# Squares' sums on VectorE, weight rests after the rows, and gates emptied in pairs, in a two-block transformer kernel

## What is computed

```python
def rmsnorm(x, g):
    return x * lax.rsqrt(jnp.mean(x * x, axis=-1, keepdims=True) + EPS) * g

# first block: start, and its end
    h = rmsnorm(x, g_mix); z = h @ w_in
    ...
    gate = jax.nn.sigmoid(rmsnorm(x, g_ple) @ w_ple_gate)
    x = x + gate * (p @ w_ple_proj)
    return rmsnorm(x, g_final)

# second block
    h = rmsnorm_2(x, norm_mix_pre)
    proj = h @ w_in
    conv_in, q, k, v, g_conv, g_att = jnp.split(proj, splits, axis=-1)
    u = causal_depthwise_conv(glu(conv_in), w, b)        # 31 taps
    u = silu(layernorm_2(u, conv_ln_g, conv_ln_b))
    att = stick_breaking_attention(q, k, v)
    merged = sigmoid(g_conv) * (u @ w_cb + b) + sigmoid(g_att) * (att @ w_ab)
```

## Time and profile before

| | us |
|---|---|
| median of 3 runs | 964.51 |
| lowest, highest | 963.71, 965.91 |
| profiled execution, own time | 964.45 |
| its span | 962.7 |
| PE busy | 935.1 (97%) |
| DVE busy | 498.7 (52%) |
| ACT busy | 330.4 (34%) |
| POOL busy | 39.2 (4%) |

### The profile page before, as it was taken

How to read it: one execution, slowest core, us unless ns; L and a number is a source line. 1 busy time by engine, 2 the same in 40 slices (tenths; PEclk the granted TensorE clock), 3 DMA queues, 4 the chain that set the end, 5 groups by cost and what they waited for, 6 DMA issues and landing times.

```text
span 962.7 us, 14239 instructions
## 1 busy us (share of the span) xinstructions
PE 935.1 (97%) x5914; PEld 660.7 (69%) x5914; DVE 498.7 (52%) x869; ACT 330.4 (34%) x527; POOL 39.2 (4%) x39
## 2 busy tenths in 40 slices
PE   7999999999999899999999899999999999999997
PEld 6997734444444444443344499988889999999886
DVE  7784613222212322222132397997788987776642
ACT  6832211001101010100011367556456755644541
POOL 1000000000000000000000000222320000000000
PEclk9999999999999999999999999999999999999999
DMA  9987799999999999999999974442334424555301
GB/s 348 403 368 325 296 396 430 428 433 429 432 428 432 427 430 430 431 432 428 431 429 419 428 302 165 176 175 88 135 129 175 176 110 176 208 211 195 132 1 44
DMA packets 28982, 289.45 MB, mean 301 GB/s; under 512 B 3057, under 2 KB 6385, under 8 KB 12401
## 3 DMA queue, kind: packets, MB, share of 16 engines
q1 hardware_dynamic: 28192, 286.91, 72.9%
q10 hardware_dynamic: 720, 1.57, 0.4%
HBM read 287.43 MB, written 1.05 MB: 300 GB/s over the span
## 4 chain that ended last, share of the span: by engine, by line
PE 82%; DVE 6%; SPq 5%; ACT 3%; DMA 2%; issue 2%; POOL 0%; DVEq 0%; ACTq 0%
PE ps L279 81%; SPq L2244 5%; DVE wl L275 3%; DMA ring<-in_w_pg 2%; ACT wh L268 1%; PE ps L1063 1%; DMA arena<-in_xT 0%; DVE arena L1549 0%; ACT arena L1848 0%; DVE arena L1889 0%; DVE arena L1960 0%; DVE mg_l L1896 0%; DVE mix_l L606 0%; ACT arena L1851 0%; DVE arena L593 0%
## 5 line engine op out<-in xcount | busy, mean ns | idle before, releaser
L279 PE MATMUL ps<-ring,arena 128*64 128x512 f32 x1216 | 339.2, 597 | 4.8 <-issue 4.7
L275 DVE TENSOR_TENSOR wl<-ring,wh 128x1024 fp32r<-128x1024 f32 x150 | 180.5, 1235 | 49.4 <-ACT wh L268 49.3
L279 PEld LDWEIGHTS ps<-ring,arena 128*64 128x64 f32 x1216 | 109.5, 137 | 122.1 <-issue 120.3
L268 ACT ACTIVATE wh<-ring 128x1024 fp32r<-128x1024 f32 x150 | 151.7, 1051 | 48.5 <-PE ps L279 34.3
L279 PE MATMUL ps<-arena 128*64 128x512 f32 (+4 forms) x448 | 166.7, 523 | 0.9 <-DMA ring<-in_moe 0.4
L279 PEld LDWEIGHTS ps<-arena 128*64 128x64 f32 (+2 forms) x448 | 58.6, 144 | 89.6 <-issue 82.8
L1168 DVE SCALAR_TENSOR_TENSOR arena<-ps,arena 128x512 f32<-128x512 f32 x16 | 12.0, 751 | 202.6 <-PE ps L279 202.6
L279 PE MATMUL ps<-up_h,wh 128*128 128x256 f32 x352 | 85.5, 281 | 0.7 <-ACT up_h L1949 0.7
L279 PE MATMUL ps<-up_l,wh 128*128 128x256 f32 x352 | 82.1, 280 | 0.0
L1238 ACT ACTIVATE y_h<-ps 128x512 fp32r<-128x512 f32 x32 | 19.0, 596 | 151.9 <-PE ps L279 151.9
L279 PEld LDWEIGHTS ps<-up_h,wh 128*128 128x128 f32 x352 | 66.3, 188 | 0.9 <-issue 0.9
(11 more groups left out here) (275 smaller groups left out, 1487.6 us busy)
## 6 DMA issues: line engine op xcount, KB each, us to landing
ring<-in_moe SPq DMA_DIRECT2D x69, 2048.0 KB, 22.5
arena<-in_moe SPq DMA_DIRECT2D x17, 2048.0 KB, 22.4
ring<-in_w_in SPq DMA_DIRECT2D x12, 2048.0 KB, 10.6
ring<-in_w_up SPq DMA_DIRECT2D x11, 2048.0 KB, 7.6
ring<-in_moe SPq DMA_DIRECT2D x24, 512.0 KB, 15.1
ring<-in_w_dn SPq DMA_DIRECT2D x5, 2048.0 KB, 7.8
ring<-in_w_out SPq DMA_DIRECT2D x4, 2048.0 KB, 16.0
arena<-in_moe SPq DMA_DIRECT2D x8, 512.0 KB, 14.6
```

Source lines behind the costliest of these rows:

```text
L268: e.activation(wh(i), raw_piece(i), ACT.Copy).then_inc(*hi.up(i))
L275: e.tensor_tensor(wl(i), raw_piece(i), wh(i), SUB).then_inc(*lo.up(i))
L279: return e.matmul(o, l, r, start=first, stop=final, skip_group_check=True)
```

## The change

1. Start: all eight sums of squares stand ahead of the first product.
2. Gate projection: `norm3`'s eight matmuls go. VectorE adds the eight chunks of `SQ` up in three steps (`added`) and PE does one matmul on the result, behind `four`. The weight rests of pieces 6 and 7 move into VectorE's loop, the reciprocal of r3 to its head, and the rests of the second projection's first four pieces from the loop to behind it.
3. Second projection: `four_late` takes the place of `four`: both products with `wh` for all rows first, then the rests of the weights. The eight `ones` matmuls go: VectorE adds the squares up into `SUM4`, and one matmul into bank 3 stands ahead of Q's products; ScalarE copies it out, and its root is taken at the merge. The weight rests 5 to 7 stand behind R45's first use.
4. Attention: two gate projections share a bank and are emptied by one operation on 512 columns; the rest of piece 41 (counted from the second projection's first) moves to the merge.
5. Merge: the mean of the convolution takes block 3 first and waits for each block by itself.

```diff
...
+        def four_late(e, outs, name, n, xh, xl, ready, at):
+            i0 = n_piece[(name, n), 0]
+            for j in range(4):
+                e.wait_ge(*hi.at(i0 + j))
+            for c in range(8):
+                e.wait_ge(*ready.at(c))
+                for j in range(4):
+                    mm(e, outs[j], wh(i0 + j)[:, c, :], xh[:, c, :], c == 0, False)
+                    mm(e, outs[j], wh(i0 + j)[:, c, :], xl[:, c, :], False, False)
+                at(e, c)
+            for j in range(4):
+                e.wait_ge(*lo.at(i0 + j))
+                for c in range(8):
+                    k = mm(e, outs[j], wl(i0 + j)[:, c, :], xh[:, c, :], False, c == 7)
+                k.then_inc(*proj.up(name, n, j))
...
-        means = sig("means", ["r1", "r3", "r4", "r5", "mu", "var", "r6", "r7"])
+        means = sig("means", ["r1", "r3", "r5", "r4", "mu", "var", "r6", "r7"])
...
             e.wait_ge(*made.at("ones"))
-            squares((1, 0, 3, 2, 5))
-            three(e, ps[3][:, 0:256], "in1", 0, 0, XGH, XGL, xg, between=lambda: squares((7, 4, 6)))
+            squares((1, 0, 3, 2, 5, 7, 4, 6))
+            three(e, ps[3][:, 0:256], "in1", 0, 0, XGH, XGL, xg)
             for j in range(1, 4):
...
         scaled = sig("scaled", range(8))
+        sum3 = sig("sum3", ["four", "two", "all"])
+        sum4 = sig("sum4", ["four", "two", "all"])
+        SUM4 = RB[:, 1, :]
         gate = sig("gate", range(8))
...
-        def sums(e, c):
+        def sum_gained(e, c):
...
             e.wait_ge(*sq4.at(c))
-            a = mm(e, ps[6][:, 0:256], inv1024, SQ[:, c, :], c == 0, c == 7)
-            b = mm(e, ps[7][:, 0:256], gsq[:, c:c + 1].to_broadcast([128, 128]), SQ[:, c, :], c == 0, c == 7)
+            k = mm(e, ps[7][:, 0:256], gsq[:, c:c + 1].to_broadcast([128, 128]), SQ[:, c, :], c == 0, c == 7)
             if c == 7:
-                a.then_inc(*means.up("r4"))
-                b.then_inc(*means.up("r5"))
+                k.then_inc(*means.up("r5"))
+        def added(e, out, ready, steps):
+            e.wait_ge(*ready.at(7))
+            e.tensor_tensor(SQ[:, 0:4, :], SQ[:, 0:4, :], SQ[:, 4:8, :], ADD).then_inc(*steps.up("four"))
+            e.wait_ge(*steps.at("four"))
+            e.tensor_tensor(SQ[:, 0:2, :], SQ[:, 0:2, :], SQ[:, 2:4, :], ADD).then_inc(*steps.up("two"))
+            e.wait_ge(*steps.at("two"))
+            e.tensor_tensor(out, SQ[:, 0, :], SQ[:, 1, :], ADD).then_inc(*steps.up("all"))
...
         def ple_pe(e):
-            def norm3(e, c):
-                mean(e, ps[7][:, 0:256], SQ, inv1024, [sq3.at(x) for x in range(8)], "r3")
-            four(e, [ps[j][:, 0:256] for j in range(4)], "pgate", 0, XPH, XPL, ple, first=ple_h, at=norm3)
+            four(e, [ps[j][:, 0:256] for j in range(4)], "pgate", 0, XPH, XPL, ple, first=ple_h)
+            e.wait_ge(*sum3.at("all"))
+            mm(e, ps[7][:, 0:256], inv1024, SQ[:, 0, :], True, True).then_inc(*means.up("r3"))
             for j in range(4, 8):
...
                                        op0=M, op1=SUB).then_inc(*ple.up(c))
-            split_lo(e, FIRST + 8)
+            added(e, SQ[:, 0, :], sq3, sum3)
+            split_lo(e, FIRST + 6)
...
             for j in range(8):
-                if j == 1:
+                if j == 0:
                     recip(e, "r3", RB[:, 0, :])
                     e.wait_ge(*recips.at("r3"))
-                if j >= 1:
+                else:
                     scale(j - 1)
+                split_lo(e, FIRST + min(6 + j, 8))
                 if j >= 2:
...
                     parts(j - 3)
-                split_lo(e, FIRST + (8, 8, 9, 10, 12, 12, 12, 12)[j])
             scale(7)
...
             parts(7)
-            split_lo(e, FIRST + 16)
+            split_lo(e, FIRST + 13)
...
         gs_in = sig("gs_in", range(4))
+        r4m = sig("r4m", [0])
         gs_sig = sig("gs_sig", range(4))
...
         at_l = h5.then(range(4))
-        sg_in = sig("sg_in", range(16))
+        sg_in = sig("sg_in", range(8))
         chunks = [(n, j) for n in range(4) for j in range(4)]
...
                     for x in range(5):
-                        sums(e, x)
-                elif c == 6:
-                    for x in range(5, 8):
-                        sums(e, x)
-            four(e, [ps[j][:, 0:256] for j in range(4)], "in2", 0, H5H, H5L, h5, at=norms)
+                        sum_gained(e, x)
+                if c >= 5:
+                    sum_gained(e, c)
+            e.wait_ge(*scaled.at(3))
+            four_late(e, [ps[j][:, 0:256] for j in range(4)], "in2", 0, H5H, H5L, h5, norms)
             for j in range(4):
-                e.wait_ge(*(scaled.at(4 + j) if j < 2 else roots.at("r4" if j == 2 else "r45")))
+                e.wait_ge(*(scaled.at(4 + j) if j < 3 else roots.at("r45")))
                 three(e, ps[4 + j][:, 0:256], "in2", 1, j, H5H, H5L)
+            e.wait_ge(*gs_in.at(3))
+            e.wait_ge(*sum4.at("all"))
+            mm(e, ps[3][:, 0:256], inv1024, SUM4, True, True).then_inc(*means.up("r4"))
             for j in range(4):
-                e.wait_ge(*gs_in.at(j))
+                e.wait_ge(*(gs_in.at(j) if j < 3 else r4m.at(0)))
                 three(e, ps[j][:, 0:256], "in2", 2, j, H5H, H5L)
...
             root(e, "r45", R45, ps[7][:, 0:256], squared=1)
-            for was in emptied(*last_in(8)):
-                e.wait_ge(*was)
-            e.wait_ge(*means.at("r4"))
-            root(e, "r4", R4, ps[6][:, 0:256])
             e.preload_act_table_set("sigmoid_and_others")
...
             for x, (dst, at) in enumerate(((IDR[:, :], C_ID), (NMR[:, :], C_NM))):
+                if x == 0:
+                    for was in emptied(*last_in(8)):
+                        e.wait_ge(*was)
                 e.activation(dst, cst[:, at:at + 128], ACT.Copy).then_inc(*masks.up(x))
+            e.wait_ge(*means.at("r4"))
+            e.activation(R4, ps[3][:, 0:256], ACT.Copy).then_inc(*r4m.up(0))
             for j in range(8):
...
                 e.tensor_tensor(GS[:, j, :], ps[j][:, 0:256], R45, M).then_inc(*gs_in.up(j))
+            split_lo(e, IN2 + 8)
+            added(e, SUM4, sq4, sum4)
             split_lo(e, IN2 + 10)
...
                 e.tensor_tensor(GS[:, j, :], GS[:, j, :], R45, M).then_inc(*gs_.up(j))
+            e.wait_ge(*sum4.at("all"))
             e.memset(CU[:, :, 0:30], 0.0).then_inc(*cpad.up(0))
...
                 n, j = chunks[g]
-                e.wait_ge(*(vv.at(g) if g < 2 else sg_in.at(g - 2)))
-                three(e, ps[j % 2][:, 0:256], "in2", 5 + n, j, H5H, H5L)
+                if g % 2 == 0:
+                    e.wait_ge(*(vv.at(g // 2) if g < 4 else sg_in.at(g // 2 - 2)))
+                three(e, ps[g // 2 % 2][:, g % 2 * 256:g % 2 * 256 + 256], "in2", 5 + n, j, H5H, H5L)
                 if g in (1, 3, 5, 7):
...
         def att_dve(e):
-            def gate(g):
-                n, j = chunks[g]
-                dst, jj = (SGC if n < 2 else SGA), 4 * (n % 2) + j
+            def gate(z):
+                n, j = chunks[2 * z + 1]
+                dst, jj = (SGC if n < 2 else SGA), 4 * (n % 2) + j - 1
                 e.wait_ge(*proj.at("in2", 5 + n, j))
-                e.tensor_tensor(dst[:, jj, :], ps[j % 2][:, 0:256], R45, M).then_inc(*sg_in.up(g))
+                e.tensor_tensor(dst[:, jj:jj + 2, :], ps[z % 2][:, :].rearrange("p (a b) -> p a b", a=2),
+                                R45.unsqueeze(1).to_broadcast([128, 2, 256]), M).then_inc(*sg_in.up(z))
...
             for g in range(16):
-                if g:
-                    gate(g - 1)
-                split_lo(e, IN2 + 20 + g + 7)
+                if g and g % 2 == 0:
+                    gate(g // 2 - 1)
+                split_lo(e, IN2 + 20 + min(g, 14) + 7)
                 if g in (3, 6, 10, 14):
...
                     softplus_dve(e, 3 + g // 2)
-            gate(15)
+            gate(7)
             taps_dve(e, 1000)
...
-            e.wait_ge(*sg_in.at(14))
-            e.wait_ge(*tap_p.at(30))
-            mean(e, ps[0][:, 0:256], CA, inv512, [tap_v.at(j, 30) for j in range(3)] + [tap_p.at(30)], "mu")
+            e.wait_ge(*sg_in.at(6))
+            for c in (3, 0, 1, 2):
+                e.wait_ge(*(tap_v.at(c, 30) if c < 3 else tap_p.at(30)))
+                k = mm(e, ps[0][:, 0:256], inv512, CA[:, c, :], c == 3, c == 2)
+            k.then_inc(*means.up("mu"))
             e.wait_ge(*at_l.at(3))
             branch(0)
-            e.wait_ge(*sg_in.at(15))
+            e.wait_ge(*sg_in.at(7))
             mean(e, ps[1][:, 0:256], TMP, inv512, [ca_sq.at(x) for x in range(4)], "var")
...
             e.preload_act_table_set("sqrt_and_others")
+            root(e, "r4", R4, R4)
             e.wait_ge(*proj.at("in2", 8, 3))
...
```

2 lines of the change are left out of this document (1 added, 1 removed).

## The result

The changed kernel takes 958.37 us (median of 4 runs, 957.93 to 959.64) against 965.21 (963.71 to 966.8) of the kernel before on the same chip. The ratio is 0.9922, its 95% interval 0.9908 to 0.9936: faster, beyond the 0.2% that can be told from no change. The forecast was 958.85 with a range of 956.6 to 961.4. It was summed against 964.45, so it forecast 5.6 us less; the medians differ by 6.8. The profiled execution of the changed kernel took 958.47 us, its span is 956.7; that is 6.0 us less than the span before.

A forecast was written before the change was run, and what follows sets the result against it. The prediction took TensorE (PE), busy 97% of the span, to bound the kernel. Its terms summed as 964.45 - 0.2 - 5.85 + 0.85 + 1.0 - 1.4 = 958.85 us, with a range of 956.6 to 961.4.

The forecast's parts named there:

- Start, -0.2: At the first product: with all eight squares' sums ahead, PE uses a 0.38 us gap and gains 0.2 us.
- Gate projection, -2.85: At the mean over SQ: 16 matmul records (3.27 us) become 2 (0.43), 2.85 us less, VectorE's additions being covered.
- Second projection, -3.0: On PE at the second projection: seven sums of 0.43 us fewer, 3.0 us less.
- Row 5, +0.85: In the second projection PE reaches h5's row 5 before VectorE has it and waits 0.85 us.
- K, +1.0: Ahead of the first attention scores PE waits 1.0 us for K(0) from VectorE; bounds none to 2.5 us.
- Tail, -1.4: At the attention stage's end, PE's 1.40 us wait for the last convolution taps goes.
- Rival 2: The attention stage's end gives nothing back, since taps beside GpSimd's additions take longer: 960.25 us, chance 0.20.
- Gates in twos, 0.1 on the path: In the attention stage, paired scalings save an estimated 0.12 us a pair, only 0.1 us on the path.
- Rival 1: PE bounds throughout and waits neither for h5's rows nor for K(0): 957.0 us, chance 0.16.
- Rival 3: VectorE is 1.5 us later at h5's rows and K(0), the end gives nothing: 963.25 us, no change, chance 0.07.
- Rival 4: VectorE bounds 558 to 628 us; all 4.8 us of additions are exposed, PE's gain waited away: 969.3 us, chance 0.03.
- point of decision: VectorE bounds once added work exceeds the waiting it can fill, 4.55 + 1.72 us and more; 4.8 is below.

The follow-up runs named there:

- the repeat: The changed kernel run and profiled once more, unchanged, on another chip: 960.16 us, ratio 0.9943 to the kernel before.
- the part alone: The kernel before with only the gates in twos, piece 41's rest behind the taps and the mean's new order: 964.70 us, ratio 0.9982.
- the gate sum alone: The kernel before with only norm3's eight matmuls replaced by three VectorE additions and one matmul, weight rests unmoved: 967.21 us, ratio 1.0017.
- aligned rows: 32 unused bytes ahead of `arena` put the rows on a multiple of 64: kernel before 956.44 us (0.9904), changed kernel 953.9 us (0.9873).

## Why the prediction was right, step by step

**Start, -0.2.** The product's rest starts at 14.27, not at 14.0; it was 14.20. The sixteen records took 6.24 us with the next product at 12.18, as forecast at 12.1. But the product behind them spread to 2.1 us where I had 1.9, since the first rounded matmul behind the sums takes 0.31 and not 0.12. In exchange the rest product no longer stands behind sums, so the next product starts at 15.21 instead of 15.33. The full pace came with the time and not with the number of records, as I had taken it: at 11.5 us behind 12 records, before at 11.8 behind 15. So 0.1 is gained at the start, and none of it is carried: the gate projection starts at 550.25 as before (550.29), since the experts' stage ahead of it goes by its loads. That their arrival cuts this term off I should have read from the profile.

**Gate projection, -2.85.** It was -3.06. The one matmul stood at 561.84 (forecast 561.98), the additions ended at 560.47 (560.5), the first scaling was at 564.77 (565.1), all as laid out. The 0.2 too much is the price of the lone sum. I had 0.43 for it; from its start to the next product's it takes 0.24 (561.84 to 562.09), as the last of the eight did before, so what went is seven times 0.43, 3.02. The other 192 products are at the same pace in both profiles, 0.1196 and 0.1194 us in the mean.

**Second projection, -3.0.** The eight sums with gsq and the one with ones took what I had for them: groups at 0.40 and 0.24 each. The groups and the switches back to products make 3.0 less, by the rows at 580.57, 584.09, 585.47 and 601.26. The interval to the scores fell by 1.4 in the result's profile and by 0.9 in the repeat's. Less the lost time at the rows (1.2, below) and at K (none, 1.1) the 3.0 would make 1.8 and 0.7. What is left is pace: before had 0.1179 us a product in the mean, the result's profile 0.1192 (0.120 from 586 to 601), the repeat 0.1175, which over 336 products is 0.4 more and 0.1 less.

**Row 5, +0.85.** The bracket says 0.56, and 0.6 in the repeat and in four more. But PE lost more than the bracket: the last product of row 4 starts at 578.67, the next was due at 578.79 and comes at 579.51, 0.7 later; and ahead of row 4 0.26 us are lost (577.35, then 577.73). Together 1.0, and 1.2 with the first product behind each, which takes 0.22 to 0.23 instead of 0.12, against 0.85; DVE's last row is there at 581.37 (forecast 581.5). A longer sum lengthened exactly this wait.

**K, +1.0.** None in the profile of the result, 1.0 in the repeat, 0.7 to 0.9 in four further kernels that have this part. So it is a term that differs among executions. What decides is how GpSimd's additions fall onto DVE's operations. From Q(0) to K(0) DVE took 12.18 us in the one and 13.19 in the repeat. The same three taps take 1.26, 1.75 or 2.24 us, with hardly any, one or two of GpSimd's additions (0.7 to 1.1 us each) running beside them, and a rest of a weight takes 1.22, 1.42 or 1.63. DVE's timeline of the changed kernel, then of the repeat, at the same instructions:

```profile
610.64 1.75 DVE L1578 SCALAR_TENSOR_TENSOR arena<-arena,vec 128x256 f32<-128x256 f32 x3
...
614.00 1.26 DVE L1578 SCALAR_TENSOR_TENSOR arena<-arena,vec 128x256 f32<-128x256 f32 x3
```
```profile
612.52 2.24 DVE L1578 SCALAR_TENSOR_TENSOR arena<-arena,vec 128x256 f32<-128x256 f32 x3
...
616.14 1.75 DVE L1578 SCALAR_TENSOR_TENSOR arena<-arena,vec 128x256 f32<-128x256 f32 x3
```

The bounds I gave, none to 2.5 with GpSimd named as the cause, held. What I did not price is that the clock can fall behind this wait: 1.7 us in two of the eight profiles that have it.

**Tail, -1.4.** -1.5 in the result, -1.6 in the repeat, -1.6 by the part alone. The taps ended at 709.76 (forecast 710.4), and PE, through with its last projection at 708.96 (forecast 709.4), had block 3 to go on with. Taking piece 41 back brought 0.6 to 0.9 again. Rival 2, whose fear was that the taps take longer, fell: 702.92 and 707.15 show 2.24 for three and 2.61 for six, so the taps beside GpSimd are the earlier ones.

**Gates in twos, 0.1 on the path.** A pair is 0.68 us long, and the next instruction starts 0.60 behind it (705.09 to 705.69); a single one stands 0.33 to 0.34 apart from the next. So a pair saves 0.07, less than the 0.12 estimated in the prediction by the Trainium skill's fixed part for PSUM sources (VectorE: DVE Perf Modes, "The TRN2 errata"). It doesn't show in the sum.

**Rivals.** Rival 1 (957.0, no waits) and the forecast (958.85) enclose the result, and its profile has one of the two waits. That the medians came within 0.5 us of the forecast is luck in part: in the profile the missing K wait (1.0 us to the good) was nearly eaten by the start (0.2), the rows (0.3) and the slower pace (0.4), and the kernel before, beside it, was 0.8 us slower than the 964.45 that I summed from. Rival 3 is out by the intervals. Rival 4, DVE as the bound: the gate sum alone came near its picture, a loss though PE had less to do, but by the weights' rests and the clock; with the whole change it's out by 11 us. Its point of decision was sound, and on aligned rows the case moves toward it.

## What to carry to other kernels

When PE is at 97%, a matmul saved is time saved only as far as the engine beside it keeps up at each place; list the waits it will meet, one by one, and expect the parts of a change to depend on each other, as the gate sum did on the second projection's part. A wait of PE can have a second price in the clock behind it (behind 3.26 us here, and behind 0.84 and 0.89 in two executions, but not behind 1.0, 2.0 and 2.2 in others), so a known small wait is worth removing; only a profile tells whether it struck. Before such edits, look at the addresses of PE's operands: 32 unused bytes were worth more here (10 us on the kernel before) than the whole change.
